# Attention of a hybrid decoder step: query tiles in another order, values with operands exchanged, a loop written out

## The reference

```python
parts = [dilated_branch_prompt(q, k, v, d, w // d) for (w, d) in ATT_BRANCHES]
out = combine_branches(parts).astype(q.dtype)     # sum_b w_b acc_b / sum_b w_b l_b
```

## Time and profile before

| | us |
|---|---|
| time, median of 3 runs | 3783.59 |
| time of the profiled execution | 3777.35 |
| its span in the profile | 3775.4 |
| TensorE busy (share of the span) | 3506.6 (93%) |
| VectorE busy | 2527.4 (67%) |
| ScalarE busy | 1309.6 (35%) |
| GpSimd busy | 1033.4 (27%) |
| first transpose of the prompt attention | 378.99 |
| last instruction group of TensorE in it starts | 714.05 |

### The profile page before, as it was taken

How to read it: one execution, slowest core, us unless ns; L and a number is a source line. 1 busy time by engine, 2 the same in 40 slices (tenths; PEclk the granted TensorE clock), 3 DMA queues, 4 the chain that set the end, 5 groups by cost and what they waited for, 6 DMA issues and landing times. The chain is left out here.

```text
span 3775.4 us, 55000 instructions
## 1 busy us (share of the span) xinstructions
PE 3506.6 (93%) x20369; PEld 2150.6 (57%) x20369; DVE 2527.4 (67%) x5185; ACT 1309.6 (35%) x2597; POOL 1033.4 (27%) x1082
## 2 busy tenths in 40 slices
PE   7998999886979998889999999999799999999997
PEld 4667666526834665446556565565355555555554
DVE  4221222214332236999999999998788988888887
ACT  3000223213201001247676776665222222222222
POOL 0000000000000000048999899996211111111110
PEclk9999555696579999999999999999899999999998
DMA  3221920355031123557878788778978878777774
GB/s 138 108 89 52 334 67 0 136 191 201 1 146 54 59 94 119 184 162 257 288 266 286 273 284 290 263 274 324 391 289 289 301 291 299 293 296 288 292 289 161
DMA packets 210413, 794.70 MB, mean 210 GB/s; under 512 B 33504, under 2 KB 92000, under 8 KB 166144
## 3 DMA queue, kind: packets, MB, share of 16 engines
q1 hardware_dynamic: 173312, 523.16, 38.4%
q0 software_dynamic: 36864, 268.45, 20.1%
HBM read 660.86 MB, written 197.66 MB: 227 GB/s over the span
## 5 line engine op out<-in xcount | busy, mean ns | idle before, releaser
L1610 PE MATMUL psum<-arena 128*128 128x400 f16 x6144 | 1097.7, 337 | 43.4 <-DVE arena L1658 42.4
L1967 PE MATMUL psum<-arena 128*128 128x400 f16 x6144 | 1049.1, 332 | 27.5 <-DVE arena L2013 27.5
L1967 PEld LDWEIGHTS psum<-arena 128*128 128x128 f16 x6144 | 596.3, 97 | 480.2 <-DVE arena L2013 27.9
L1610 PEld LDWEIGHTS psum<-arena 128*128 128x128 f16 x6144 | 597.3, 99 | 471.7 <-DVE arena L1658 53.0
L1582 POOL TENSOR_SCALAR arena<-arena 128x128 f16<-128x128 f16 x800 | 712.7, 904 | 50.7 <-DVEq L1788 26.3
L115 POOL DMA_INDIRECT arena<-in_experts,arena x256 | 300.7, 1175 | 1177.0 <-DVE arena L148 1080.8
L134 ACT ACTIVATE arena<-arena 128x1 f32<-128x1 f32 x256 | 51.5, 201 | 922.4 <-DVE arena L127 922.3
L148 DVE SCALAR_TENSOR_TENSOR arena<-arena 128x1024 f32<-128x1024 f32 x256 | 330.7, 1292 | 18.3 <-issue 2.8
L2020 DVE TENSOR_TENSOR arena<-arena,psum 128x800 f32<-128x800 f32 x256 | 252.2, 985 | 107.4 <-PE psum L1967 107.4
L127 DVE CUSTOM_DVE_ANT_0 arena<-arena 128x1024 f32<-128x1024 f32 x256 | 311.5, 1219 | 18.1 <-DMA arena<-in_experts,arena 17.1
L1839 ACT ACTIVATE arena<-arena 128x128 f16<-128x128 f16 x800 | 245.1, 388 | 87.3 <-DVE arena L1796 82.4
(11 more groups left out here) (234 smaller groups left out, 3863.9 us busy)
## 6 DMA issues: line engine op xcount, KB each, us to landing
arena<-in_u_feat SPq DMA_DIRECT2D x128, 512.0 KB
arena<-in_experts SPq DMA_DIRECT2D x128, 512.0 KB, 4.8
scratch_acts<-arena SPq DMA_DIRECT2D x128, 400.0 KB
arena<-scratch_gates SPq DMA_DIRECT2D x32, 1600.0 KB
arena<-scratch_acts SPq DMA_DIRECT2D x128, 400.0 KB, 6.1
scratch_gates<-arena SPq DMA_DIRECT2D x48, 1024.0 KB
out_k_win_sample<-in_cache_k SPq DMA_DIRECT2D x32, 1022.0 KB, 29.4
out_v_win_sample<-in_cache_v SPq DMA_DIRECT2D x32, 1022.0 KB, 32.2
```

The source lines that it names most:

```text
L1610: last = pe.matmul(psum[:, 2 * p + k, 0:SLD], w[:, s, q, :], xs[:, q, k * SLD:(k + 1) * SLD], start=q == 0 and w is u_hi and xs is x_hi, s ...
L1967: last = pe.matmul(psum[:, 2 * (n % BANKS) + i, 0:SLD], w[:, s, k, q * P:(q + 1) * P], hs[:, s, k, i * SLD:(i + 1) * SLD], start=k == 0 an ...
```

## The change

The order of a pair's query tiles becomes 0, 7, 1, 6, 2, 5, 3, 4. The values product exchanges its operands: the head's values (64 columns) are the weights, the transposed probabilities (128 columns) move, and the result has the head's 64 features on partitions and a query on each column, in the half of the output bank's partitions that belongs to the head. The output transpose and its copy go. In their place the reciprocals of the row sums are put on the diagonal of a 128 x 128 tile (`share`, VectorE), and a product with 64 columns of ones spreads them over the 64 partitions (TensorE, behind the values); VectorE copies that out of PSUM and multiplies, straight into the mixed features. The `Fori` loops become plain loops that are written out, and the `settled` increments behind waits on register values go.

```diff
-        tile = [n // 2 % TT for n in range(BLOCKS)]
+        turn_of = (0, 7, 1, 6, 2, 5, 3, 4)
+        tile = [turn_of[n // 2 % TT] for n in range(BLOCKS)]
...
-            with pe.Fori(0, H // 2 // PAIRS) as turns:
+            for turns in range(H // 2 // PAIRS):
...
                     for k in range(i + 1):
-                        last = pe.matmul(psum[:, 6 + n // 2 % 2, 64 * half:64 * half + 64],
+                        last = pe.matmul(psum[64 * half:64 * half + 64, 6 + n // 2 % 2, 0:P],
+                                         at(V0 + k * 512 + turns * (PAIRS * P) + pair * P + 64 * half, 64),
                                          turned[:, n % 2, k * P:(k + 1) * P],
-                                         arena[:, bass.ds(V0 + k * 512 + turns * (PAIRS * P) + pair * P + 64 * half, 64)],
                                          start=k == 0, stop=k == i)
-                    last.then_inc(values_ready, 1)
-
-                def turn_out(t):
-
-                    pe.wait_ge(out_scaled, turns * TILES + t + 1)
-                    pe.transpose(psum[:, 6 + t % 2, P:2 * P], out_tok[:, t % 2, :], m["ident"]).then_inc(out_turned, 1)
+
+                    pe.wait_ge(share_ready, turns * BLOCKS + n + 1)
+                    pe.matmul(psum[64 * half:64 * half + 64, 6 + n // 2 % 2, P:2 * P], m["ones"][:, 0:64],
+                              shares[:, n % 2, :], start=True, stop=True).then_inc(values_ready, 1)
...
+                def share(n):
+
+                    dve.wait_ge(exp_ready, turns * BLOCKS + n + 1)
+                    dve.wait_ge(values_ready, turns * BLOCKS + n + 1)
+                    dve.reciprocal(inv[:, n // 2 % 2, n % 2:n % 2 + 1], total[:, n // 2 % 2, n % 2:n % 2 + 1])
+                    dve.drain()
+                    dve.tensor_scalar(shares[:, n % 2, :], m["ident"], inv[:, n // 2 % 2, n % 2:n % 2 + 1], None,
+                                      ALU.mult).then_inc(share_ready, 1)
+
                 def scale_out(t):
-
+                    pair, i = t // TT, tile[2 * t]
                     dve.wait_ge(values_ready, turns * BLOCKS + 2 * t + 4)
-                    dve.sem_inc(settled["dve"], 1)
-                    dve.reciprocal(inv[:, t % 2, :], total[:, t % 2, :])
+                    dve.tensor_copy(spread[:, t % 2, :], psum[:, 6 + t % 2, P:2 * P])
                     dve.drain()
-                    dve.tensor_tensor(out_tok[:, t % 2, :].rearrange("p (h d) -> p h d", h=2),
-                                      psum[:, 6 + t % 2, 0:P].rearrange("p (h d) -> p h d", h=2),
-                                      inv[:, t % 2, :].unsqueeze(2).broadcast_to([P, 2, 64]),
-                                      ALU.mult).then_inc(out_scaled, 1)
+                    dve.tensor_tensor(at(XT0 + i * P + pair * T + turns * (PAIRS * T), P), psum[:, 6 + t % 2, 0:P],
+                                      spread[:, t % 2, :], ALU.mult).then_inc(out_copied, 1)

                 for n in range(BLOCKS):
                     add_bias(n)
+                    if n >= 1:
+                        share(n - 1)
                     if n >= 3 and n % 2 == 1:
                         scale_out(n // 2 - 1)
+                share(BLOCKS - 1)
                 scale_out(TILES - 1)
```

More of the change, by code:

```diff
@@ L408, in attend_prompt @@
 def attend_prompt(nc, x, m, kv_out, windows_shifted):
-    psum, at, arena = m["psum"], m["at"], m["arena"]
+    psum, at = m["psum"], m["at"]
     with ExitStack() as c:
@@ L419, in attend_prompt @@
         pair_k = at(word, 2, SEQ); word += 2 * SEQ
-        out_tok = at(word, 2, P); word += 2 * P
+        shares = at(word, 2, P); word += 2 * P
+        spread = at(word, 2, P); word += 2 * P
         top = at(word, 2, 1); word += 2
@@ L434, in attend_prompt @@
         values_ready = sem("values_ready")
-        out_scaled = sem("out_scaled")
-        out_turned = sem("out_turned")
+        share_ready = sem("share_ready")
         out_copied = sem("out_copied")
-        settled = {e: sem(f"settled_{e}") for e in ("pe", "act", "dve")}
         block = c.enter_context(nc.Block())
@@ L477, in scores @@
                         pe.wait_ge(pair_staged, turns * (2 * PAIRS) + 2 * pair + 2)
-                        pe.sem_inc(settled["pe"], 1)
                     pe.wait_ge(scores_read, turns * BLOCKS + n + 1)
-                    pe.sem_inc(settled["pe"], 1)
                     width = (i + 1) * P
@@ L526, in _ @@
                         values(n - 1)
-                    if n >= 3 and n % 2 == 1:
-                        turn_out(n // 2 - 1)
                 values(BLOCKS - 1)
-                turn_out(TILES - 1)
         @block.vector
@@ L536, in _ @@
             dve.wait_ge(bias_loaded, 16)
-            with dve.Fori(0, H // 2 // PAIRS) as turns:
+            for turns in range(H // 2 // PAIRS):
                 def add_bias(n):
@@ L575, in _ @@
             act.sem_inc(values_ready, 2)
-            with act.Fori(0, H // 2 // PAIRS) as turns:
+            for turns in range(H // 2 // PAIRS):
                 def exps(n):
@@ L586, in copy_pieces @@
                     act.wait_ge(values_ready, turns * BLOCKS + n + 1)
-                    act.sem_inc(settled["act"], 1)
                     for b in range(pieces[n]):
@@ L592, in copy_pieces @@
                                  psum[:, 4 + (before[n] + b) % 2, 0:e - s]).then_inc(piece_copied, 1)
[L594 to L599, removed]
                 for n in range(BLOCKS):
@@ L604, in _ @@
                         copy_pieces(n - 1)
-                    if n >= 4 and n % 2 == 0:
-                        copy_out(n // 2 - 2)
                 copy_pieces(BLOCKS - 1)
-                copy_out(TILES - 2)
-                copy_out(TILES - 1)
 def hgrn(nc, x, m, windows_shifted):
```

## The result

The changed kernel takes 3672.16 us (median of 4 runs, 3669.52 to 3675.92) against 3784.69 us (four runs of the kernel before beside them): a ratio of 0.9709, 95% interval 0.9689 to 0.9729. 3668 was forecast. The profiled execution took 3669.52 us with a span of 3667.4.

What follows compares the result with a forecast made beforehand. TensorE at half clock was taken to bound the 335.5 us attention. Pieces 169, joints 23, new joints 10, slow start 7, VectorE 1 and waits 13 gave 223 us, 112 less; forecast 3668 us, range 3640 to 3700.

Steps and rivals of the forecast that it cites:

- The term that decides: TensorE's clock in the attention: rises from 1.2 to 2.4 GHz in the first visit to tile 7 and stays.
- count of full feeds: TensorE passes per key chunk in the attention that are a full feed: 1 of 5 before, 3 of 5 after.
- the 7 that I had: Attention's first 15 us at half clock, priced at 7 us extra.
- The pieces: TensorE's 128-column pieces in the attention: 1472 + 96 = 1568 at 0.108 us each, 169 us at 2.4 GHz.
- The joints: TensorE's changes of array shape in the attention: 64 x 0.36 = 23 us, plus 10 us for new joints.
- The new one: Shape change between transposes and values: 0.15 us each, 10 us over 64 blocks at full clock.
- The waits: TensorE's waits for exponentials and piece copies at large tiles: 3.2 us per head pair, 13 us in all.
- The first block of tile 7: TensorE waits 0.6 us for this block's exponentials before its first transpose.
- The ones: Product spreading the reciprocals in the attention: 64 products of two passes each, 128 pieces added.
- Nothing behind took it back: Rival: sample attention's loads wait for the window copies and use up the gain, 3777 us; 4 in 100.
- A clock that stays low: Rival: attention's clock stays at 1.2 GHz, attention 380 us, kernel 3821 us; 1 in 10.
- One that goes up and down: Rival: clock raised by value stretches, lost in scores, transposes and small tiles; 3743 us; 11 in 100.

Runs made afterwards that it cites:

- e1: Kernel before with only the query tile order changed to 0, 7, 1, 6, 2, 5, 3, 4: 3788.26 us, ratio 1.0005.
- e3: Kernel before with only the loop written out and the increments behind register waits gone: 3782.34 us, ratio 0.9978.
- e2: Changed kernel with the old query tile order (0, 0, 1, 1 up to 7, 7) put back: 3667.49 us, ratio 0.9687.
- e4: Kernel before with each value pass moving both heads' 128 columns in place of 64, half the result unused: 3668.24 us, ratio 0.9689.
- e10: Kernel before with score products taking all 128 partitions, so the heads are not separated: 3645.36 us, ratio 0.9643.
- e6: Changed kernel with its four head pairs in one sequence of 64 blocks, no drain between two turns: 3668.88 us, ratio 0.9699.
- e5: Changed kernel without the ones product and TensorE's wait for the shares, normalisation left out: 3658.34 us, ratio 0.967.

## Why the prediction was right

**The clock.** The term that decides was right in size and in mechanism: neither the order (e1) nor the loop (e3) raises the clock, the gain is there without the new order (e2), and the values' moving operand alone raises it (e4). That the scores can do the same (e10) fits the prediction's count of full feeds: 3 of 5 passes in e4, in e10 and in the changed kernel, 1 of 5 before. That it is the feed remains argued. Right in part was the course: I had the clock rise some 15 us after the start (18.5 measured) and hold to the end. It fell once, for 6.9 us at the border between the turns, where TensorE waited 1.6 us for the first exponentials of a tile 0 and then had scores of tile 7; e6 removes it:

```profile
493.81 0.33 PE L493 MATMUL psum<-consts,arena 128*128 128x128 f32 x1 [1.61 <-ACT arena L576]
494.06 1.98 PE L481 MATMUL psum<-arena 64*128 64x512 f32 x4
```

Work at half clock was 18.3 + 6.9 = 25.2 us, which costs 12.6 us against the 7 that I had.

**The pieces.** 0.108 us held for the exchanged product: fourteen passes of tile 6 from 409.92 to 411.49, 1.57 us, are fourteen times 0.108 and 0.06 more, which is part of the joint in front of them. Timeline of TensorE:

```profile
405.74 0.98 PE L493 MATMUL psum<-consts,arena 128*128 128x128 f32 x7
406.65 0.65 PE L503 MATMUL psum<-arena 128*64 128x128 f32 x4
407.14 0.38 PE L509 MATMUL psum<-arena,consts 128*64 128x128 f32 x2
407.45 0.91 PE L481 MATMUL psum<-arena 64*128 64x384 f32 x2
409.03 0.95 PE L493 MATMUL psum<-consts,arena 128*128 128x128 f32 x7 [0.67 <-ACT arena L586]
409.92 1.74 PE L503 MATMUL psum<-arena 128*64 128x128 f32 x14
411.49 0.38 PE L509 MATMUL psum<-arena,consts 128*64 128x128 f32 x2
411.81 0.91 PE L481 MATMUL psum<-arena 64*128 64x384 f32 x2
```

**The joints.** The new one, transposes to values, was taken at 0.15 us. Read record by record, passes of one kind start 0.109 us apart here; the first value of 409.92 starts 0.202 behind the last transpose, and the second value 0.160 behind the first: together 0.14 above the pace. In e4, where the shape does not change between the two (tile 6, first value at 417.55), the same two steps are 0.109 and 0.112, no joint. The Trainium skill (TensorEngine Tiling, Key Properties) says that a change of tiling mode drains TensorE; the trace agrees, with 0.14 us at this joint. All joints together: TensorE's busy time at full clock, 93.45 + 93.47 + 25.2/2 = 199.5, less 169.3 for the 1568 pieces, is 30 us; the sum had 23 + 10 = 33.

**The waits.** 13 us forecast, 11.6 + 7.5 - 10.0 = 9.1 measured. They do not stand where I put most of them. The first block of tile 7, priced at 0.6 us, shows no wait for its exponential. Inside a turn TensorE waits only at the second half of tiles 4, 6 and 7, 0.67 us at tile 6 (409.03) and up to 1.31 at tile 7, each time for a copy of pieces (L586): these transposes need a PSUM bank that holds pieces of the block before, and ScalarE copies those only behind the exponential of the block itself. ScalarE ahead of 409.03, and TensorE at the tile 7 of the second pair:

```profile
407.28 1.04 ACT L576 ACTIVATE arena<-arena 128x896 f32<-128x896 f32 x1 [1.52 <-DVE arena L537]
408.32 0.95 ACT L586 COPY arena<-psum 128x512 f32<-128x512 f32 x2
448.05 1.06 PE L493 MATMUL psum<-consts,arena 128*128 128x128 f32 x8 [1.31 <-ACT arena L586]
```

**The ones.** Priced at 14 us by their pieces; taking them out is worth 9.5, an earlier rise of the clock included, because what they occupy is partly time in which the chain over ScalarE would be late (5.7 us in e5). As the worth of an edit, a price by pieces was too high by that.

**Nothing behind took it back.** The sample attention's first product waited 9.8 us for its keys before and 10.0 after, as forecast, and the sum of the terms, 223 us, met 222.3 (379.2 to 601.5). That it met so closely is in part luck: half clock cost 5.6 us more than its term, and waits and joints came out 4 and 3 us below theirs. The time came out 4 us above 3668, which is less than the spread of the first expert stage.

**The rivals.** A clock that stays low did not come in any run of an edit that fills the feed. One that goes up and down is what e4 shows, where small tiles stand together, and even there 3668 us; in e2, with the same order of tiles, it fell only between the turns. By the rule on transposes that the Trainium skill states (TensorE: Matmul & The Clock Gate, Part 4) the prediction gave the changed kernel such a course, with 3743 us; the trace has 2.4 GHz over 197 of 222 us.

## What to carry to other kernels

When TensorE is busy all the time and its granted clock reads 0.50, look at what moves as well as at waits. Here the kernel with scores fed from 64 partitions and value passes of 64 columns behind a load of 128 had 1.2 GHz, and changing either of the two gave 2.4 GHz over most of the attention. Try the small test first, moving columns that nobody uses in time that the weight load takes anyway; a value pass took 0.112 us in e4 and 0.107 to 0.112 at the same clock before, and the test gave the whole 3%. Price waits from the stage at its new speed, since an edit that frees TensorE hands part of it back to the chain behind.

## What the runs showed of the hardware that was not expected

A few runs of e1 and e3 stand apart from the rest in mean granted clock and time. Of ten runs of e1 nine had a mean granted clock of 0.904 to 0.906 and 3784.86 to 3792.79 us, and one 0.915 and 3753.25 us; one of ten of e3 had 0.920 and 3732.39 us, the others 0.903 to 0.909. None of the 19 runs of the kernel before beside them shows it (0.904 to 0.908). The two quicker ones have no profile, so that it was the attention which ran faster in them is not shown.
